# A SwiGLU feed-forward in three parts of its inner rows, each with its own pass over the output tiles

## The reference, cut to what matters

```python
D_MODEL, DEPTH, D_FF = 1024, 2, 2816

def _swiglu(h, w_in, w_out):
    gate, up = jnp.split(h @ w_in, 2, axis=-1)
    return (jax.nn.silu(gate) * up) @ w_out

for i in range(DEPTH):
    ...                                   # x += mixer(rmsnorm(x))
    xp = xp + _swiglu(_rmsnorm(xp, norm_ffn[i]), ffn_w_in[i], ffn_w_out[i])
    xs = xs + _swiglu(_rmsnorm(xs, norm_ffn[i]), ffn_w_in[i], ffn_w_out[i])
y_prompt, y_sample = _rmsnorm(xp, norm_final), _rmsnorm(xs, norm_final)
```

## Time and profile before

| | |
|---|---|
| median of 3 runs | 1629.31 us (1628.5 to 1630.7) |
| span of the profiled execution | 1627.6 us |
| TensorE busy with matmuls | 1571.9 us, 97% |
| VectorE, ScalarE, GpSimd busy | 613.6, 604.4, 605.6 us (38, 37, 37%) |
| mean granted TensorE clock | 0.984 |
| DMA | 123.76 MB, 76 GB/s on average |

### The profile page before, as it was taken

One profiled execution on the slowest core, in us unless ns is written; L12 is line 12 of the kernel. 1 busy time (PEld: TensorE's weight loads), 2 busy tenths in 40 slices (PEclk: granted clock), 3 DMA queues, 4 the chain that ended last, 5 costly groups with the idle time before them and its releaser, 6 DMA issues.

```text
span 1627.6 us, 29919 instructions
## 1 busy us (share of the span) xinstructions
PE 1571.9 (97%) x11071; PEld 1484.0 (91%) x11071; DVE 613.6 (38%) x1075; ACT 604.4 (37%) x1059; POOL 605.6 (37%) x292
## 2 busy tenths in 40 slices
PE   6999999999999999999999999999999999999996
PEld 6778888899999999999978888888999999999996
DVE  5566666553111111121355666565431111111212
ACT  5466666543222222222334444444342222222221
POOL 3333334234445444433322222222344544544331
PEclk9899999999999999999999999999999999999998
DMA  4122112112222222222221111211122222222222
GB/s 164 61 74 81 63 60 71 56 65 78 81 87 77 86 82 77 82 85 84 91 82 61 61 60 60 63 56 47 65 66 89 77 81 87 77 84 78 81 84 81
DMA packets 41555, 123.76 MB, mean 76 GB/s; under 512 B 4624, under 2 KB 9232, under 8 KB 41504
## 3 DMA queue, kind: packets, MB, share of 16 engines
q1 hardware_dynamic: 41504, 123.06, 22.5%
HBM read 111.21 MB, written 11.83 MB: 76 GB/s over the span
## 4 chain that ended last, share of the span: by engine, by line
PE 86%; DVE 6%; issue 3%; ACT 3%; DMA 0%; SPq 0%; POOL 0%; DVEq 0%; ACTq 0%; POOLq 0%
PE ps L487 70%; PE sps L537 3%; PE ops L600 2%; PE tps L557 2%; PE sps L543 2%; PE sps L539 2%; PE sps L538 2%; DVE qf L1242 1%; PE sps L545 1%; PE ops L590 1%; DVE acc L1200 1%; ACT qsw L836 1%; DVE qf L1215 1%; PE tps L571 1%; DVE aug_l L1328 1%
## 5 line engine op out<-in xcount | busy, mean ns | idle before, releaser
L1096 POOL TENSOR_TENSOR w_lo<-w_raw,w_hi 128x1024 fp32r<-128x1024 f32 (+1 forms) x199 | 470.9, 2367 | 851.5 <-ACT w_hi L796 851.5
L487 PE MATMUL ps<-xh,w_hi 128*128 128x288 f32 x2176 | 491.5, 308 | 20.8 <-DVE xl L1443 11.8
L487 PE MATMUL ps<-xh,w_lo 128*128 128x288 f32 x2176 | 470.0, 298 | 0.0
L487 PE MATMUL ps<-xl,w_hi 128*128 128x288 f32 x2176 | 469.7, 298 | 0.0
L796 ACT ACTIVATE w_hi<-w_raw 128x1024 fp32r<-128x1024 f32 (+1 forms) x200 | 208.3, 1042 | 451.9 <-PE ps L487 449.4
L487 PEld LDWEIGHTS ps<-xh,w_hi 128*128 128x128 f32 x2176 | 351.8, 192 | 22.9 <-issue 22.1
L487 PEld LDWEIGHTS ps<-xh,w_lo 128*128 128x128 f32 x2176 | 354.5, 191 | 0.0
L487 PEld LDWEIGHTS ps<-xl,w_hi 128*128 128x128 f32 x2176 | 354.2, 191 | 0.0
L887 ACT ACTIVATE pr<-sps,nmax 128x384 f32<-128x384 f32 (+3 forms) x160 | 86.0, 538 | 189.1 <-DVE nmax L1258 171.7
L487 PE MATMUL ps<-hh,w_lo 128*128 128x288 f32 x704 | 150.9, 295 | 0.0
L487 PE MATMUL ps<-hl,w_hi 128*128 128x288 f32 x704 | 150.8, 295 | 0.0
(11 more groups left out here) (155 smaller groups left out, 1845.7 us busy)
## 6 DMA issues: line engine op xcount, KB each, us to landing
w_raw<-w_units SPq DMA_DIRECT2D x184, 512.0 KB, 3.2
w_raw<-w_units SPq DMA_DIRECT2D x16, 384.0 KB, 2.9
xT<-x_in SPq DMA_DIRECT2D x8, 288.0 KB, 5.7
dk_out<-kf SPq DMA_DIRECT2D x8, 288.0 KB, 2.1
dv_out<-vf SPq DMA_DIRECT2D x8, 288.0 KB, 4.0
fk_out<-kf SPq DMA_DIRECT2D x8, 288.0 KB, 4.1
fv_out<-vf SPq DMA_DIRECT2D x8, 288.0 KB, 4.0
y_out<-yt SPq DMA_DIRECT2D x8, 288.0 KB, 2.3
```

The lines of the kernel that those rows point to most:

```text
L487: mm = nc.tensor.matmul(out[:, half, :], w[:, k, :], rhs[:, kt, half * HALF:(half + 1) * HALF], start=start and w is w_hi[slot] and rhs is ...
L1096: nc.gpsimd.tensor_tensor(w_lo[slot][:, 0:kts, :], w_raw[slot][:, 0:kts, :], w_hi[slot][:, 0:kts, :].bitcast(F32), ALU.subtract).then_inc( ...
```

## The change

Before, a layer's feed-forward runs all 44 gate and up units and then 24 output units, three for each of 8 output tiles. Now the 22 inner tiles are dealt with in three parts of 8, 8 and 6. Each part runs its gate and up units (16, 16, 12), and then 8 output units, one for each output tile, over the part's inner tiles alone (8, 8 or 6 slices). Each output unit is a PSUM accumulation of its own and is added to `xT` on its own, so that there are 24 `residual` additions in a layer where there were 8. `prep` runs after the third part's additions only. The units, their contents and the matmuls are the same; their order, and so the order of the loads, splits and `w_lo`, is another. SyncE's `load_unit` gets an argument `of`, the unit's place in HBM, which is as before. The buffers keep their sizes. Each engine's two loops of a layer become six.

```diff
-N_WO, N_IN, N_OUT, N_LAYER = 24, 36, 80, 88
+N_WO, N_IN, N_LAYER = 24, 36, 104
+UP = [sum(2 * n + KT for n in OUT_PARTS[:p]) for p in range(4)]
+PART_AT = [sum(OUT_PARTS[:p]) for p in range(3)]
@@ SyncE
-                with sp.Fori(0, FT) as it:
-                    for s in range(2):
-                        load_unit(Num(U_LAYER * L + U_IN + s, 2, it))
-                with sp.Fori(0, KT // 2) as it:
-                    for s in range(6):
-                        load_unit(Num(U_LAYER * L + U_OUT + s, 6, it), OUT_PARTS[s % 3])
+                for p, tiles in enumerate(OUT_PARTS):
+                    u = U_LAYER * L + U_IN
+                    with sp.Fori(0, tiles) as it:
+                        for s in range(2):
+                            load_unit(Num(u + UP[p] + s, 2, it), of=Num(u + 2 * PART_AT[p] + s, 2, it))
+                    with sp.Fori(0, KT // 2) as it:
+                        for s in range(2):
+                            load_unit(Num(u + UP[p] + 2 * tiles + s, 2, it), tiles,
+                                      of=Num(U_LAYER * L + U_OUT + 3 * s + p, 6, it))
@@ TensorE
-                def out_tile(u, n, first):
-                    for part, kts in enumerate(OUT_PARTS):
-                        open_unit(u + part, n, tile=part == 0)
-                        for k in range(kts):
-                            kt = KT * part + k
-                            if first:
-                                pe.wait_ge(hl_done, val(FT * L + kt + 1))
-                            mm = slice_(u + part, n, k, hh, hl, kt, kt == 0, kt == FT - 1)
-                        mm.then_inc(w_used, 1)
+                def out_unit(u, n, p, first):
+                    open_unit(u, n)
+                    for k in range(OUT_PARTS[p]):
+                        kt = PART_AT[p] + k
+                        if first:
+                            pe.wait_ge(hl_done, val(FT * L + kt + 1))
+                        mm = slice_(u, n, k, hh, hl, kt, k == 0, k == OUT_PARTS[p] - 1)
+                    mm.then_inc(w_used, 1)
+
+                in_unit(u + 1, n + 1)
+                for p, tiles in enumerate(OUT_PARTS):
+                    skip = 1 if p == 0 else 0
+                    with pe.Fori(0, tiles - skip) as it:
+                        for s in range(2):
+                            in_unit(Num(u.c + UP[p] + 2 * skip + s, 2, it), Num(n.c + UP[p] + 2 * skip + s, 2, it))
+                    for k in range(2):
+                        out_unit(u + (UP[p] + 2 * tiles + k), n + (UP[p] + 2 * tiles + k), p, k == 0)
+                    with pe.Fori(0, KT // 2 - 1) as it:
+                        for s in range(2):
+                            at_ = UP[p] + 2 * tiles + 2 + s
+                            out_unit(Num(u.c + at_, 2, it), Num(n.c + at_, 2, it), p, False)
@@ ScalarE (gate_up: lead(u + 1, cols), Silu, lead(u + 2, cols), hh, as before; cols is the next units' width)
-                def out_tile(n, u, last):
-                    lead(u + 1, OUT_PARTS[2])
+                def out_unit(p, k, last):
+                    u = k + (U_LAYER * L + U_IN + UP[p] + 2 * OUT_PARTS[p])
                     if not last:
-                        lead(u + 2)
-                        lead(u + 3)
-                    act.wait_ge(ps_read, val(n + (N_LAYER * L + N_OUT + 1)))
-                    prep(2 * L + 2, n)
+                        lead(u + 1, OUT_PARTS[p] if k.c < KT - 2 else KT)
+                    if p == 2:
+                        act.wait_ge(ps_read, val(k + (N_LAYER * L + N_IN + UP[p] + 2 * OUT_PARTS[p] + 1)))
+                        prep(2 * L + 2, k)
+                for p, tiles in enumerate(OUT_PARTS):
+                    ...
+                    gate_up(p, Num(tiles - 1), tiles)
+                    if p == 2:
+                        act.preload_act_table_set("natural_log_exp_and_others")
@@ GpSimd (gate_up: lead(u + 1, cols), lead(u + 2, cols), hf, as before)
+                for p, tiles in enumerate(OUT_PARTS):
+                    ...
+                    gate_up(p, Num(tiles - 1), tiles)
+                    u = U_LAYER * L + U_IN + UP[p] + 2 * tiles
+                    with pool.Fori(0, KT // 2 - 1) as it:
+                        for s in range(2):
+                            lead(Num(u + s + 1, 2, it), tiles)
+                    for k in range(KT - 2, KT):
+                        if L == DIFF or p < 2:
+                            lead(Num(u + k + 1))
@@ VectorE (gate_up: take gf, take uf, hl, as before)
-                clear_acc(2 * L + 2)
-                with dve.Fori(0, KT // 2) as it:
-                    for s in range(2):
-                        k = Num(s, 2, it)
-                        dve.wait_ge(w_used, val(Num(U_LAYER * L + U_OUT + 3 * (s + 1), 6, it)))
-                        residual(k + (N_LAYER * L + N_OUT), k)
-                        prep(2 * L + 2, k)
+                for p, tiles in enumerate(OUT_PARTS):
+                    ...
+                    if p == 2:
+                        clear_acc(2 * L + 2)
+                    with dve.Fori(0, KT // 2) as it:
+                        for s in range(2):
+                            k = Num(s, 2, it)
+                            dve.wait_ge(w_used, val(k + (U_LAYER * L + U_IN + UP[p] + 2 * tiles + 1)))
+                            residual(k + (N_LAYER * L + N_IN + UP[p] + 2 * tiles), k)
+                            if p == 2:
+                                prep(2 * L + 2, k)
```

More of the change, by code:

```diff
@@ L41 @@
 U_WO, U_IN, U_OUT, U_LAYER = 24, 32, 76, 100
-N_WO, N_IN, N_OUT, N_LAYER = 24, 36, 80, 88
+N_WO, N_IN, N_LAYER = 24, 36, 104
+UP = [sum(2 * n + KT for n in OUT_PARTS[:p]) for p in range(4)]
+assert U_IN + UP[3] == U_LAYER and N_IN + UP[3] == N_LAYER
+PART_AT = [sum(OUT_PARTS[:p]) for p in range(3)]
 WO_STEPS = ([(j, 2 + j, k) for j in (0, 1) for k in range(6)] + [(0, 2, 6), (1, 3, 6)]
@@ L359, in _, with load_unit @@
         def _(sp):
-            def load_unit(u, cols=KT):
+            def load_unit(u, cols=KT, of=None):
                 slot = u.c % 2
+                of = u if of is None else of
                 if u.it is None and u.c == 2:
@@ L368, in load_unit @@
                     sp.wait_ge(w_lo_done, val(u - 1))
-                if u.it is None or u.k == 0:
-                    src = w_units[u.c]
+                if of.it is None or of.k == 0:
+                    src = w_units[of.c]
                 else:
-                    src = w_units[bass.ds(u.v(), 1)].rearrange("a p n -> (a p) n")
+                    src = w_units[bass.ds(of.v(), 1)].rearrange("a p n -> (a p) n")
                 sp.dma_start(w_raw[slot][:, 0:cols, :], src[:, 0:cols * P].rearrange("p (k n) -> p k n", n=P)
@@ L746, in _ @@
                 first_unit(u, n, prep_count(L, 1, 0), 2 * L + 1).then_inc(w_used, 1)
-                open_unit(u + 1, n + 1)
-                for k in range(KT):
-                    mm = slice_(u + 1, n + 1, k, xh, xl, k, k == 0, k == KT - 1)
-                mm.then_inc(w_used, 1)
-                with pe.Fori(0, FT - 1) as it:
-                    for s in range(2):
[L753 to L757, removed]
@@ L769, in _, with in_unit @@
[L769 to L774, removed]
+                def in_unit(u, n):
+                    open_unit(u, n)
+                    for k in range(KT):
+                        mm = slice_(u, n, k, xh, xl, k, k == 0, k == KT - 1)
+                    mm.then_inc(w_used, 1)
@@ L1050, in _, with gate_up @@
                 scale_of_norm(2 * L + 1)
[L1052 to L1055, removed]
+                def gate_up(p, i, cols=KT):
+                    jt = i + PART_AT[p]
+                    j, u, n = jt + FT * L, i * 2 + (U_LAYER * L + U_IN + UP[p]), i * 2 + (N_LAYER * L + N_IN + UP[p])
+                    lead(u + 1, cols)
                     act.wait_ge(ps_read, val(n + 1))
@@ L1059, in gate_up @@
                     nc.scalar.activation(sg[:], gf[:], ACT.Silu).then_inc(sg_done, 1)
-                    lead(u + 2)
+                    lead(u + 2, cols)
                     act.wait_ge(hf_done, val(j + 1))
@@ L1063, in gate_up @@
                     nc.scalar.activation(at(hh, jt), hf[:], ACT.Copy).then_inc(hh_done, 1)
[L1065 to L1068, removed]
-                def out_tile(n, u, last):
-                    lead(u + 1, OUT_PARTS[2])
-                    if not last:
-                        lead(u + 2)
-                        lead(u + 3)
-                    act.wait_ge(ps_read, val(n + (N_LAYER * L + N_OUT + 1)))
-                    prep(2 * L + 2, n)
[L1078 to L1083, removed]
+                def out_unit(p, k, last):
+                    u = k + (U_LAYER * L + U_IN + UP[p] + 2 * OUT_PARTS[p])
+                    if not last:
+                        lead(u + 1, OUT_PARTS[p] if k.c < KT - 2 else KT)
[3 more added lines that the diff above has]
+                for p, tiles in enumerate(OUT_PARTS):
+                    skip = 1 if p == 0 else 0
+                    if skip:
```

(55 more changed lines are left out.)

1 line of the change is left out of this document (removed).

## The result

The changed kernel takes 1641.49 us (median of 5 runs, 1639.28 to 1643.72) against 1629.67 us for the kernel before (5 runs, 1628.5 to 1636.37). The ratio is 1.0066, with a 95% interval from 1.0048 to 1.0084: slower by 11.8 us, clear of no change. The profiled execution has a span of 1640.1 us, 12.5 us more than the one of before.

What follows compares the result with a forecast made beforehand. TensorE's dense matmuls were taken to bound the kernel; stalls of 11.5 us plus a clock fall of 1.5 made 13.0 us on a 1627.6 us span, 1640.6, plus 1.7 for timed runs: 1642.3 us, range 1639 to 1648.

Steps and rivals of the forecast that it cites:

- the chain that was named: Behind each part's last up unit: `w_hi`, `w_lo`, `hf`, `hh`, `hl`, ending 6.92 us after the first output matmul.
- the pace of 0.1333 us a matmul: TensorE's dense feed-forward stretches: 3132 matmuls in 417.6 us, expected to stay at this pace between the waits.
- The stalls: TensorE waits for `hl` in each part's first output unit: 1.63, 1.63 and 2.47 us a layer, 11.5 us in all.
- The reaction of 0.24 us: Time from VectorE's end to TensorE's matmul, read at the attention output's residual and applied to `hl`.
- One fall after two long stalls: TensorE's clock drops to half once behind the two part-three stalls: 1.5 us, with 0 and 3.0 as bounds.
- Residuals and PSUM reads: 16 further VectorE additions a layer, 0.76 us each, hidden in idle time: nothing; 24 us without that cover.
- Seams: Six loops per engine in place of two, some 8 more TensorE seams a layer: nothing; 20 us from above.
- `prep` in part three: Layer 0: a tile's VectorE chain takes about 4.0 of the 4.8 us available, so it fits narrowly.
- Rival 2: Not slower, 1629.3 us: the chain behind the last up unit ends before TensorE needs it; chance 0.03.
- All six falls (1): The clock falls after every one of the six stalls: 20.5 us, giving 1649.8 us; chance 0.05.
- seams (3): The further loop seams cost TensorE time, up to 20 us, giving 1662 us; chance 0.03.
- late VectorE (4): VectorE falls behind in part three of layer 0, the layer ending 5 us late: 1647 us; chance 0.03.

Runs made afterwards that it cites:

- experiment 1: Changed kernel, but in each part's last gate and up pair GpSimd multiplies `hf` before the second `w_lo`; 1626.45 us, ratio 0.9981 to the kernel before.
- experiment 2: Changed kernel with all gate and up pairs first, then the 24 output units part by part; 1630.62 us, ratio 0.9999 to the kernel before.
- experiment 3: Changed kernel with one further GpSimd product ahead of `hf` in each part's last pair; 1648.01 us, ratio 1.0107 to the kernel before.
- experiment 6: Kernel before with TensorE's gate and up loop cut into three loops with the same body; 1629.14 us, ratio 1.0006.
- experiment 5: Changed kernel with `hf` ahead of the second `w_lo` and two attention residuals ahead of preparations; 1624.19 us, ratio 0.9971 to the kernel before.
- experiment 4: Kernel before with the attention residuals of output tiles 6 and 7 moved ahead of the preparations of tiles 5 and 6; 1625.25 us, ratio 0.9965.

## Why the prediction was right

**What bounds, and where it can be lost.** TensorE bounds the feed-forward and lost its time at the six places that were named, each behind the chain that was named; experiments 1, 2 and 3 show the cause. Wrong was that no time could be won: the prediction held the pace of 0.1333 us a matmul for fixed. The first profile has it throughout, but in the second one the second layer's feed-forward runs in part at 0.1300 us and takes 419.54 us, 1.9 us over the kernel before in place of 4.9.

**The stalls.** The mechanism and the number of them were right, the size was over by 0.28 us each: 1.35 and 2.18 us measured, 1.63 and 2.47 forecast, 9.8 us in all in place of 11.5. Two terms were off. The reaction of 0.24 us was taken from a wait for a residual; for `hl` it is 0.05 us (`hl` ends at 480.49, the matmul starts at 480.54). And the chain is 0.12 us shorter, 6.80 us from the first output matmul at 473.68 to 480.48: from `hf` to `hh` it is 1.46 us (477.42 to 478.88) where it was 1.55. The last pair of a part is written outside ScalarE's and GpSimd's loops now, where it was inside before. The traces show that the two go together: in all eleven profiles the step from `hf` to `hh` is 1.43 to 1.47 us for a pair that is written outside the loops (the first of a layer and, in the kernels in three parts, the last of a part) and 1.55 to 1.57 us for one inside. What in a loop costs the 0.1 us is open. The first pair after the stall cost 0.10 us, not 0.07.

**The clock.** One fall after two long stalls was forecast, and the first profile has exactly that. In the second one both long stalls have it. The one was a choice between 0 and 2, and that it fitted the first profile was luck. With 1.35 us no stall had it in either; in experiment 3 two of the four stalls of 2.7 us had it, and one of the two of 3.5 us. The length of a stall alone doesn't tell whether the clock falls.

**What was costed at nothing.** Residuals and PSUM reads: shown by experiment 2. Seams: shown by experiment 6 for pure ones; for those between output and gate units, by the changed kernel's own chain, which goes through them without a wait. `prep` in part three: a tile's chain of 4.0 us was forecast, and it is 771.58 to 775.59, 4.01 us; the last residual starts at 800.38, 4.81 us after the one before it, so it isn't late. VectorE's timeline of the changed kernel, one tile of it:

```profile
771.58 0.76 DVE L1221 TENSOR_TENSOR xT<-ps,xT 128x576 f32 x1 [1.65 <-PE ps L497]
773.65 1.28 DVE L1207 SCALAR_TENSOR_TENSOR xl<-xT,smalls,xh  x1 [1.31 <-ACT xh L824]
774.85 0.74 DVE L1212 TENSOR_TENSOR acc<-acc,sqt 128x576 f32<-128x576 f32 x1
```

**The sum.** 9.8 + 1.5 = 11.3 us in the feed-forwards, where 13.0 was forecast. 1.2 us came from elsewhere and hid a part of the error: the second layer's attention took 402.33 us in place of 400.76. The granted clock is 0.50 in both windows of 4 us from 836 to 844 and 0.74 in the next; the kernel before does the same work 6 us earlier and has 0.61 and 0.96 in the two windows from 832 to 840 and 1.00 in the next. The fall at 1188 us was missing in return. The attention's code is the same; why its falls came otherwise was not settled. So the forecast of 1642.3 us met 1641.49 by errors that cancel in part, and by an execution without the quicker pace. The second measurement is only 7.7 us above its kernel before, and its median of 1638.33 us lies just below the stated range, which began at 1639. The term that is missing from the sum is the pace: it was put at nothing, and it was worth 4.4 us in that profile.

**The rivals.** All six falls (1), seams (3) and a late VectorE (4) didn't come. Rival 2's condition, `hf` ahead of the `w_lo`, was built as experiment 1. Its price for parts one and two was right, for part three it was 1.06 us and not nearly 0.6, since I had not counted that the `w_lo`, moved behind `hf`, would hold `hl`.

## What to carry to other kernels

When a consumer is moved right behind its producer, count the whole chain between them in the program order of every engine, and hold it against the consumer's first use of the newest piece; one item that may wait and stands ahead of one that may not is a cheap thing to exchange. Here 24 further microseconds of busy time on an idle engine (32 x 0.757) cost nothing, and 1.25 us of lateness cost 1.35 us four times over. After such an exchange look at the moved item's new neighbour, too: here it held the next link of the same chain.

## What the runs showed of the hardware

TensorE ran at two dense paces at full clock, for the same 128x288 matmuls with a weight load each: 133.3 and 130.0 ns (in the profiles of experiments 1, 3 and 5 and the second one of the changed kernel). In the feed-forwards the quicker one was seen only after a change from output units to gate units, and held until the change back to output units; of 12 feed-forwards with such changes 7 had it somewhere, of 10 without (the kernel before twice, experiments 2, 4 and 6) none. It is worth up to 4.5 us a layer and differs between executions of one kernel. What sets it stays open, and how often the timed executions have it isn't known, so the part of experiment 1's gain that comes from it is argued, not shown.

In the two profiles of the changed kernel the granted clock fell at three of the four stalls of 2.2 us and at none of the eight of 1.35 us. The attention of the first layer began its half-clock stretches otherwise in the three profiles of experiments 1 and 5 that have `hf` first, and was 5 us longer there, with the same code in it. It was 4 to 6 us shorter than in the other profiles in those of experiment 6 and the second one of the changed kernel, again with the same code. What sets it is open too.
